# Larger diagonal blocks in the triangular inverse of a gated delta rule: 16x16 on VectorE instead of 8x8, and one doubling level fewer on TensorE

## What is computed

```python
# chunks of 64 positions, 8 of them; kb = k * beta, decay is lower triangular
L = jnp.where(strict, jnp.einsum('bhnid,bhnjd->bhnij', kb, k) * decay, 0.0)
u = lax.linalg.triangular_solve(L, v * beta[..., None], left_side=True, lower=True, unit_diagonal=True)
w = lax.linalg.triangular_solve(L, kb * jnp.exp(g)[..., None], left_side=True, lower=True, unit_diagonal=True)
...
def step(state, inp):
    v_new = u_c - jnp.einsum('bhcd,bhde->bhce', w_c, state)
    o = jnp.einsum('bhcd,bhde->bhce', qd, state) + jnp.einsum('bhij,bhje->bhie', a_c, v_new)
    state = state * jnp.exp(gl)[..., None, None] + jnp.einsum('bhcd,bhce->bhde', kd, v_new)
    return state, o
```

## Time and profile before

| | |
|---|---|
| device time, median of 3 runs | 2406.57 us (2405.77 to 2411.68) |
| the profiled execution | 2409.68 us |
| its span in the profile | 2407.9 us |
| TensorE busy / weight loads | 97% / 79% of the span |
| VectorE, ScalarE, GpSimd busy | 52%, 45%, 48% |
| mean granted TensorE clock | 0.992 |

### The profile page before, as it was taken

The page is one execution under the profiler, slowest core; times in us unless marked ns, Lnnn a source line. Parts: engine busy times, 40 slices in busy tenths (PEclk is TensorE's granted clock), DMA queues, the critical chain, the costliest instruction groups (busy, mean ns, idle before and its releaser), DMA issues.

```text
span 2407.9 us, 33566 instructions
## 1 busy us (share of the span) xinstructions
PE 2343.6 (97%) x13052; PEld 1891.1 (79%) x13052; DVE 1256.6 (52%) x2464; ACT 1073.1 (45%) x2287; POOL 1148.7 (48%) x844
## 2 busy tenths in 40 slices
PE   8999899999999999999999999999999999999998
PEld 6777777778888888877878777788877888777886
DVE  5877864663441111278777546634496511565152
ACT  6566543443343323255666434443532332434442
POOL 3343334334666556543333333356665564634464
PEclk9999999999999999999999999999999999989999
DMA  4111112222322222321111121223224333353322
GB/s 151 62 62 54 45 53 70 71 71 79 97 79 96 96 97 96 100 68 62 54 53 62 49 76 62 71 83 112 70 98 135 126 105 97 111 179 124 98 94 79
DMA packets 76510, 207.31 MB, mean 86 GB/s; under 512 B 16704, under 2 KB 27712, under 8 KB 75840
## 3 DMA queue, kind: packets, MB, share of 16 engines
q1 hardware_dynamic: 76352, 205.18, 26.4%
HBM read 194.66 MB, written 10.49 MB: 85 GB/s over the span
## 4 chain that ended last, share of the span: by engine, by line
PE 82%; DVE 10%; ACT 3%; POOL 2%; issue 1%; DMA 0%; SPq 0%; DVEq 0%; ACTq 0%
PE ps L987 23%; PE ps L989 22%; PE ps L988 22%; PE ps L2015 1%; PE ps L1943 1%; PE ps L2027 1%; PE ps L1966 1%; POOL wL L941 1%; PE ps L1962 1%; DVE ctw L1205 1%; PE ps L2021 1%; DVE ctmp L1205 1%; ACT prob L1468 1%; ACT wH L934 1%; PE ps L1992 1%
## 5 line engine op out<-in xcount | busy, mean ns | idle before, releaser
L941 POOL TENSOR_TENSOR wL<-raw,wH 128x512 fp32r<-128x512 f32 x660 | 903.2, 1390 | 1047.6 <-ACT wH L934 1047.3
L934 ACT ACTIVATE wH<-raw 128x512 fp32r<-128x512 f32 x660 | 379.5, 623 | 727.2 <-PE ps L989 723.6
L987 PE MATMUL ps<-hH,wH 128*128 128x512 f32 x1584 | 654.5, 413 | 1.7 <-POOL wL L941 1.7
L989 PE MATMUL ps<-hH,wL 128*128 128x512 f32 x1584 | 621.7, 392 | 0.0
L988 PE MATMUL ps<-hL,wH 128*128 128x512 f32 x1584 | 620.3, 392 | 0.0
L987 PEld LDWEIGHTS ps<-hH,wH 128*128 128x128 f32 x1584 | 299.2, 189 | 67.0 <-issue 9.1
L989 PEld LDWEIGHTS ps<-hH,wL 128*128 128x128 f32 x1584 | 298.7, 189 | 65.4
L988 PEld LDWEIGHTS ps<-hL,wH 128*128 128x128 f32 x1584 | 299.7, 189 | 51.1 <-issue 0.7
L987 PE MATMUL ps<-OH,wH 128*128 128x512 f32 x576 | 227.6, 395 | 6.9 <-POOL OL L2097 2.4
L989 PE MATMUL ps<-OH,wL 128*128 128x512 f32 x576 | 224.4, 390 | 0.0
L988 PE MATMUL ps<-OL,wH 128*128 128x512 f32 x576 | 224.4, 390 | 0.0
(11 more groups left out here) (430 smaller groups left out, 3441.5 us busy)
## 6 DMA issues: line engine op xcount, KB each, us to landing
raw<-w SPq DMA_DIRECT2D x345, 512.0 KB, 3.3
mats<-matsD SPq DMA_DIRECT2D x4, 1408.0 KB, 6.8
x<-xT SPq DMA_DIRECT2D x8, 256.0 KB, 6.3
matsD<-Cd SPq DMA_DIRECT2D x8, 256.0 KB, 2.6
matsD<-wide SPq DMA_DIRECT2D x4, 512.0 KB, 3.4
mats<-lagsD SPq DMA_DIRECT2D x32, 64.0 KB, 5.7
outT<-acc SPq DMA_DIRECT2D x8, 256.0 KB, 2.2
matsD<-tab SPq DMA_DIRECT2D x8, 128.0 KB, 1.9
```

Of the source, the lines that this page charges most:

```text
L934: act.activation(weights_at(slot)[0][:, k, :], raw[:, n % RAW, k, :], ACT.Copy).then_inc(high_done, 1)
L941: pool.tensor_tensor(low[:, k, :], raw[:, n % RAW, k, :], high[:, k, :].bitcast(F32), ALU.subtract).then_inc(low_done, 1)
L987: pe.matmul(out, wh, rH[:, t, :], start=(t == 0), stop=False)
L989: mm = pe.matmul(out, wl, rH[:, t, :], start=False, stop=(t == depth - 1))
```

## The change

`PACK` goes from 8 to 16, and `LEVELS` from (8, 16, 32) to (16, 32). The planner's assumed duration of a `solve` step goes from 0.5 to 0.68 us. The third hunk only lets two-digit names such as `solve14` find their branch. Everything else follows from the two constants: V has 64 columns instead of 32, a head has 14 solve steps instead of 6 and two doubling levels instead of three, and the planner writes a new order for all engines in both layers.

```diff
-PACK = 8
-LEVELS = (8, 16, 32)
+PACK = 16
+LEVELS = (16, 32)
...
-               ("D", "first"): 0.9, ("A", "pack"): 0.55, ("A", "solve"): 0.5, ("A", "minus"): 0.6, ...
+               ("D", "first"): 0.9, ("A", "pack"): 0.55, ("A", "solve"): 0.68, ("A", "minus"): 0.6, ...
...
-                        elif kind == "A" and (s[:-1] in ("pmask", "update", "flip", "solve") or s in ("pack", "minus", "negate")):
+                        elif kind == "A" and (s[:-1] in ("pmask", "update", "flip") or s.startswith("solve") or s in ("pack", "minus", "negate")):
```

## The result

The changed kernel takes **2516.36 us** (2515.11 to 2517.19) where the kernel before takes 2406.22 in the same comparison: ratio 1.0446, 95% interval 1.043 to 1.0463. It is slower by 110 us, where the prediction had 35 and a range that ended 79 us above. The profiled executions differ by as much: spans of 2513.3 and 2407.9 us.

What follows compares the result with a forecast made beforehand. TensorE was taken to set the pace, about level with the inverse chain. Level -21.4, runs +48, old idle -15.9, clock +15, other waits 4 us per layer: +34, rounded to +35, so 2442 us, range 2405 to 2485.

Steps and rivals of the forecast that it cites:

- Level gone, -21.4: TensorE, both layers: one doubling level of three removed, a third of lines 1962 and 1966, saves 21.4 us.
- A solve step at 0.80 us: VectorE: a solve step of 64 columns takes 0.80 us instead of 0.69, bounds 0.69 and 0.90.
- Price of the listed runs, +48: TensorE's queue: idle in long runs of small groups without weight matmuls, 28 us first layer, 20 second; bounds 25 and 80.
- The clock, +15: TensorE at half clock after sparse runs: 3 more such spells than now, +15 us, bounds 0 and 30.
- Waits outside the list, +8: Shorter runs in TensorE's queue: waits behind a VectorE at 90%, 4 us per layer.
- idle of before: TensorE in the two inverse stretches: the present idle time, 15.9 us, all replaced by the new order, so -15.9.
- Places of the loss: Inverse stretches: 50 to 70 us with no matmul, in the places of the runs of 17, 19 and 18.
- VectorE at 85 to 90%: Sign in the changed profile: VectorE's busy share in the two stretches from first pack to last negate.
- rival 3: Inverse stretches: VectorE becomes the bound for good, about +70, 2477 us; chance 0.17 for over 2465.
- 48 us per layer: VectorE: time added by the longer solve less one level's steps, 5.9 us per head; bounds 34 and 60.
- Cross-check by the chain, 18 to 50 us: Inverse chain: ends 24 to 40 us later per layer, less slack, so 18 to 50 us in both layers.
- slack of 15 us per layer: Ahead of tile ya 0, which first needs head 7's output: 15 us per layer of chain delay absorbed.

Runs made afterwards that it cites:

- e3: The kernel before in its own order, 8x8 blocks, with the first doubling level left out: 2395.76 us, ratio 0.9939.
- e12: e11 plus two matmuls that nobody reads ahead of 40 small groups in TensorE's long runs: 2546.31 us, ratio 1.0566.
- e1: The changed kernel's work (16x16 blocks, 14 solve steps, two levels) in the order planned for the kernel before: 2456.26 us, ratio 1.0195.
- e8: The changed kernel planned anew with factor 0.9 instead of 1.25 on VectorE, ScalarE and GpSimd durations, heads 0 to 5: 2437.33 us, ratio 1.0127.
- e15: The changed kernel planned anew with factor 1.0 instead of 1.25 on those engines' durations, heads 0 to 5: 2438.24 us, ratio 1.0119.
- e2: The changed kernel in its own order, 8 of 14 solve steps per head replaced by a four-element copy: 2519.24 us, ratio 1.0447.
- e18: The changed kernel planned with factor 0.9 for inverse-related steps and q, k, v, z tiles of heads 1 to 5, 1.25 elsewhere except last heads: 2436.08 us.
- e10: e8 with 8 of the 14 solve steps per head replaced by a four-element copy: 2417.85 us, ratio 1.0036.
- e7: The kernel before, own order and three levels, with 14 solve steps of 32 columns instead of 6: 2480.9 us, ratio 1.0288.
- e16: The changed kernel planned anew with factor 1.4 instead of 1.25 on VectorE, ScalarE and GpSimd durations, heads 0 to 5: 2547.8 us, ratio 1.0573.
- e19: The changed kernel planned with factor 1.25 for the weight tiles' own chains and 1.0 for D, A and B of heads 0 to 5: 2466.94 us.
- e11: The changed kernel in its own order with V in SBUF instead of PSUM: 2546.54 us, ratio 1.0567.

## Why the prediction was right or wrong

- **Direction: right.** The level removed from TensorE is worth less than what the longer solve and the new order cost.
- **Level gone, -21.4: over-valued.** TensorE's busy time fell by 19.9 us in e3, the time by 15. Almost six microseconds had been filling gaps; the sum counted them as path.
- **A solve step at 0.80 us: right.** Two steps of after start 381.70 - 380.90 = 0.80 us apart, at 225 to 232 ns an instruction:

```profile
380.90 0.23 DVE L1617 STREAM_SHUFFLE solve_rows<-ps 128x64 f32<-128x64 f32 x1
...
381.70 0.23 DVE L1617 STREAM_SHUFFLE solve_rows<-ps 128x64 f32<-128x64 f32 x1
```

- **Price of the listed runs, +48: right in sum, in part by luck.** The idle time of a tile is its length less TensorE's busy time. In the first layer the tiles with the runs of 13, 11, 17 and 19 have 7.4, 1.8, 7.3 and 4.8 us, 21 where the sum had 28. In the second those with the runs of 9, 18, 10 and 11 have 6.0, 8.4, 7.9 and 2.0 us, 24 where it had 20. Together this is 46 us. The run of 19 was priced far too high (13 us), and that made up for others that were priced too low. The tiles not shown above are tile 30 of the first layer and tiles 18, 30 and 37 of the second; the last row is tile 22 of the first layer, whose run has only 6 groups:

```profile
282.40:294.80 12.40, 10.62 (x59) 8.64 (x58) 11.31 (x52) 9.85 (x30) 2.50 (x2) 1.00 0.12 44
1212.70:1239.60 26.90, 20.89 (x137) 17.02 (x137) 14.14 (x33) 10.54 (x31) 5.43 (x4) 0.68 0.06 20
1360.30:1387.70 27.40, 19.52 (x138) 15.45 (x137) 16.89 (x39) 15.13 (x36) 3.94 (x3) 0.69 0.06 20
1451.90:1469.20 17.30, 15.30 (x131) 11.05 (x131) 7.48 (x22) 7.53 (x17) 3.78 (x3) 1.00 0.10 31
189.40:213.30 23.90, 16.28 (x96) 12.40 (x94) 15.20 (x42) 14.25 (x33) 3.76 (x3) 0.64 0.07 23
```

- **The clock, +15: the step that failed, and the largest error.** TensorE's busy time between tiles 9 and 44 holds 57 us of it. The sum had three spells more than before, of ten microseconds each. The clock records of after have 13 spells there, of up to 20.5 us, together 167 us against 10 before. How much of this is a loss of its own isn't settled: TensorE might have waited longer at full clock, and in the run of 18 the half clock cost nothing (e12).
- **Waits outside the list, +8: the other step that failed.** TensorE is idle 82.4 us between tiles 9 and 44; 46 lie in the tiles of the list, 37 elsewhere. The sum took the length of a run as the measure and gave the shorter ones 4 us per layer. Tile 22 of the first layer has 7.6 us idle, as much as the tile with the run of 17. One step in its run waits 5 us for VectorE, and all groups and the weight tile stand behind it:

```profile
197.26 1.12 PE L1986 MATMUL ps<-cst,U 128*128 128x128 f32 x4 [5.08 <-DVE U L1666]
```

- **The sum once more, with what was measured** between tiles 9 and 44: -21.4 (level) + 45.6 (listed runs) + 36.8 (other waits) - 17.8 (idle of before) + 57.1 (busy time, half clock) = 100 us, where the prediction's terms gave +34. Of the missing 66 us the clock is 42 and the other waits are 29 (the rest takes some 4 off). These are entries of an account, and no independent causes; the cause that the runs show is the order, which moves all of them at once (e1, e8, e15).
- **Places of the loss: right for the most part.** Of the nine longest tiles of after the prediction had named seven by their runs (17, 13, 19, 10, 9, 18 and 8 groups), the last without a price. It had not named tile 22 of the first layer and tile 26 of the second, with 6 groups each, at 23.9 and 21.1 us. And the two runs of 11 have next to no idle time (1.8 and 2.0 us) and the full clock.
- **VectorE at 85 to 90%, rival 3: wrong.** It stood at 71 and 69%. The 48 us per layer counted steps from start to start, gaps included, while busy time rose by 70 us in both layers together, 35 per layer; that would still be 84 to 86% of the old stretches. And cutting eight steps changed nothing (e2). The total of 2516 lies beyond rival 3's 2477, but not by its mechanism: the stretch grew faster than VectorE's load.
- **Cross-check by the chain, 18 to 50 us: wrong.** The stretches grew by 60 and 61 us, not 24 to 40. Probably the chain's own links waited in the queues too; no run shows this by itself. The slack of 15 us per layer can't be read off any run.
- **What the change costs in the best orders tried.** It is 25 to 28 us (e8, e15, e18). With the level at -15, the added VectorE work costs some 41 us gross, for 52 to 62 us more of busy time. In the order of e8, eight of its steps are worth 20 us (e10); in e7's order steps cost their full time. How the rest divides between VectorE's load and waits wasn't separated, and an order that nobody tried may be better. The forecast of +35 comes near this size by luck, since it was added up for the order with the long runs, in which the loss is some 80 us more.

I took the planner's order as given and priced its runs one by one, when a second look was at hand: the order could have been written with other factors before any run. The growth of the runs from 9 to 19 groups was a warning, though run length alone, as e16 and e19 show, doesn't tell a good order from a bad one. Why the planner does better with a smaller factor stays open too: its 0.68 x 1.25 = 0.85 us for a solve step is nearer to the measured 0.80 than 0.68 x 0.9 = 0.61.

## What to carry to other kernels

When a change alters the assumed durations or the number of steps in a statically planned kernel, measure the same instructions under two or three other settings of the planner before judging the change: here one constant moved the time by 110 us, four times the 25 to 28 that the change costs in the best orders tried. A stretch in which all engines have gaps and each wait of TensorE names another releaser points to the order; here, work taken off VectorE brought nothing there (e2). Don't price an order by its longest runs alone: in a short run, too, one late step holds up all that stands behind it. Removed work can have filled gaps; only the part that lay on the path comes back (15 of 21 us in e3).

## What the hardware showed that I had not expected

Moving V from PSUM to SBUF gave the two tensor_tensor instructions of a step two inputs in SBUF. Most of them cost as before, but the mean rose from 225 and 232 ns to 345 and 382. The trace of e11, by tile (count: duration in ns, least/median/most):

```profile
L1618 DVE TENSOR_TENSOR solve_rows<-packed,solve_rows x224: 224/226/1310, 78.6 to 1516.3; 128x64 f32<-128x64 f32 x112
L1619 DVE TENSOR_TENSOR packed<-packed,solve_rows x224: 224/225/1310, 78.9 to 1516.6; 128x64 f32<-128x64 f32 x112
```

Of the 448 instructions 74 took over 300 ns. Every one of them started while GpSimd was in an instruction, and ended 0.08 us after that instruction ended. Two in a row, with GpSimd's below (the x2 are two instructions back to back, to 1260.62):

```profile
1258.57 0.91 DVE L1618 TENSOR_TENSOR solve_rows<-packed,solve_rows 128x64 f32<-128x64 f32 x1
1259.52 1.19 DVE L1619 TENSOR_TENSOR packed<-packed,solve_rows 128x64 f32<-128x64 f32 x1
...
1258.13 2.49 POOL L941 TENSOR_TENSOR wL<-raw,wH 128x512 fp32r<-128x512 f32 x2 [2.96 <-ACT wH L934]
```

The two rows are busy 60 us more than in after, and this kernel was 30 us slower. The Trainium skill (SBUF — State Buffer, Who interferes with whom) states that VectorE with two SBUF inputs and a GpSimd instruction that reads SBUF take turns, and that the later one waits for the whole instruction of the other; the trace agrees, with waits of up to 1.1 us. The convolution taps (two SBUF inputs, 512 elements) show it in the kernel before too, and in after: one took 1.16 us where the next took 0.74, and ended 0.55 us after GpSimd's L941 (1247.68 + 2.49 = 1250.17):

```profile
1249.56 1.16 DVE L1779 SCALAR_TENSOR_TENSOR ks<-tmp,par,ks 128x511 f32<-128x511 f32 x1
...
1251.57 0.74 DVE L1779 SCALAR_TENSOR_TENSOR ks<-tmp,par,ks 128x510 f32<-128x510 f32 x1
```

In e2 the same tap started 0.84 us earlier, took 1.75 us and ended only 0.25 us earlier, by as much as GpSimd's instruction did. In this place VectorE time that was set free came to nothing:

```profile
1248.72 1.75 DVE L1782 SCALAR_TENSOR_TENSOR ks<-tmp,par,ks 128x511 f32<-128x511 f32 x1
```
